# A two-layer mixture of experts on one core: expert 0's rows chosen ahead of the full choice, gate ahead of up for experts 0 and 31, the last down matrix in two halves

## What is computed

```python
g = argmax(h @ w_group + b_group)              # 4 groups of 8 experts
vals, loc = top_k((h @ w_expert + b_expert)[group g], 2)
gates = softmax(groups)[g] * softmax(vals)
for each token's two experts e:
    y += gate * ((silu(x @ w_gate[e]) * (x @ w_up[e])) @ w_down[e])
```

## Time and profile before

| what | value |
| --- | --- |
| median of 3 runs | 1813.89 us (1813.64 to 1815.15) |
| the profiled execution, its own time | 1813.51 us |
| its span in the profile | 1811.8 us |
| TensorE busy | 1522.4 us (84%) |
| VectorE busy | 931.3 us (51%) |
| ScalarE, GpSimd busy | 166.1 us (9%), 111.8 us (6%) |
| read from memory | 531.89 MB, 297 GB/s over the span |
| TensorE's granted clock, mean of the span | 0.918 |

### The profile page before, as it was taken

One profiled execution on the slowest core, in us unless ns is written; L12 is line 12 of the kernel. 1 busy time (PEld: TensorE's weight loads), 2 busy tenths in 40 slices (PEclk: granted clock), 3 DMA queues, 4 the chain that ended last, 5 costly groups with the idle time before them and its releaser, 6 DMA issues. The chain is left out here.

```text
span 1811.8 us, 32599 instructions
## 1 busy us (share of the span) xinstructions
PE 1522.4 (84%) x14545; PEld 1022.8 (56%) x14545; DVE 931.3 (51%) x1882; ACT 166.1 (9%) x388; POOL 111.8 (6%) x121
## 2 busy tenths in 40 slices
PE   8998858788877799876666666689999999999998
PEld 6655534454444795543333333379699445779843
DVE  5844334543234684433322212388877553886756
...
DMA  9377999999999858899999999926544434435420
GB/s 331 140 311 331 414 384 426 426 427 427 427 427 411 327 192 338 351 426 427 426 426 427 426 428 428 415 102 233 186 165 162 168 107 166 140 117 195 154 92 24
DMA packets 80186, 540.33 MB, mean 298 GB/s; under 512 B 7374, under 2 KB 9486, under 8 KB 54188
## 3 DMA queue, kind: packets, MB, share of 16 engines
...
HBM read 531.89 MB, written 6.29 MB: 297 GB/s over the span
## 5 line engine op out<-in xcount | busy, mean ns | idle before, releaser
L930 PE MATMUL ps<-ring,work 128*32 128x256 f32 x3968 | 323.0, 497 | 233.6 <-DMA ring<-in_moe_w_up 231.0
L930 PEld LDWEIGHTS ps<-ring,work 128*32 128x32 f32 x3968 | 177.5, 142 | 373.6 <-issue 338.9
L2372 DVE TENSOR_TENSOR rowb<-rowb,ps 128x128 f32<-128x128 f32 x64 | 18.4, 287 | 381.8 <-ACT rowb L1740 381.8
L906 PE MATMUL ps<-ring,work 128*128 128x512 f32 x312 | 139.5, 592 | 0.0
L942 PE MATMUL ps<-ring,multi 128*32 128x256 f32 x1920 | 114.7, 379 | 0.1
L906 PEld LDWEIGHTS ps<-ring,work 128*128 128x128 f32 x312 | 59.0, 190 | 72.7 <-issue 72.7
L1440 PE MATMUL ps<-hT,ring 128*128 128x128 f32 x768 | 95.4, 275 | 1.5 <-ACT hT L1655 1.5
L906 PE MATMUL ps<-work 128*128 128x512 f32 x212 | 96.0, 592 | 0.0
L1440 PEld LDWEIGHTS ps<-hT,ring 128*128 128x128 f32 x768 | 90.4, 192 | 2.0 <-ACT hT L1655 2.0
L1740 ACT ACTIVATE rowb<-ps 128x128 f32<-128x128 f32 x64 | 17.7, 277 | 753.4 <-PE ps L930 753.4
L963 PE MATMUL ps<-hres,rowb 128*32 128x256 f32 (+1 forms) x1280 | 86.5, 385 | 0.0
...
## 6 DMA issues: line engine op xcount, KB each, us to landing
...
```

Source lines behind the costliest of these rows:

```text
L906: mm = pe.matmul(ps[:, product_bank[n][i], :], left[:, k, :], right[:, k, :], start=(j == 0 and k == 0), stop=(j == pieces - 1 and k == 1))
L930: mm = pe.matmul(ps[32 * q:32 * q + 32, bank, 0:256].rearrange("p (u n) -> p u n", u=2), x[:, k, :], gu[:, k, :, P * q:P * q + P], start=( ...
L2372: link(V.tensor_tensor(hid[b], silu[b], ps[:, 4 + b, P:2 * P], ALU.mult))
```

## The change

1. **Expert 0 ahead of the choice.** Which rows go to expert 0 is found from the logits alone: group 0 is the largest, and expert 0's logit is at least the second largest of its group. VectorE gets this by `max` (the eight largest of a row), three comparisons and products (signal `choice`, first count). TensorE ranks that one column (`running_ranks`, 3, 2 and 1 columns), VectorE makes expert 0's 0/1 matrix, and only then goes on to the full choice, which is rewritten with `max` and fewer passes. The full ranks and totals (`all_ranks`) stand after expert 0's products on TensorE, and the later ranking on VectorE after expert 0's silu product. Expert 1's rows are now picked after expert 0's down product, and their transpose is the last thing in `route`.
2. **Gate ahead of up.** For experts 0 and 31 `gate_or_up` does the gate product and then the up product, 32 matmuls of 128 columns each instead of 32 of 256 in all. Expert 0's gate slot is released after the gate product (`gate_up` counts one more from there on). Expert 31's gate product no longer waits for the up matrix.
3. **The last down matrix in two halves.** Expert 31's down matrix is loaded by two transfers of 1 MB, and the first half of its product waits for the first alone.
4. `keep_busy` goes from 8 (layer 1: 7) to 1 after the logits, from 4 to none behind the ranks, and from 5 to 3 ahead of expert 31 of layer 0.

```diff
-                    holder[s] = (("down" if kind == "down" else "gate_up") + str(l), e + 1)
+                    holder[s] = (f"down{l}", e + 1) if kind == "down" else (f"gate_up{l}", 1 if (e, kind) == (0, "gate") else e + 2)
...
+                    if (e, kind) == (NE - 1, "down"):
+                        sp.dma_start(dst[:, 0:SLOT // 2], src[:, 0:SLOT // 2]).then_inc(S("early_down"), 16)
+                        dst, src = dst[:, SLOT // 2:], src[:, SLOT // 2:]
                     sp.dma_start(dst, src).then_inc(done, 16)
...
+            def gate_or_up(x, bank, gu, u, chunks=range(DC)):
+
+                for k in chunks:
+                    for q in range(4):
+                        mm = pe.matmul(ps[32 * q:32 * q + 32, bank, P * u:P * u + P], x[:, k, :], gu[:, k, u, P * q:P * q + P],
+                                       start=(k == 0), stop=(k == DC - 1))
+                return mm
...
-                keep_busy(8 if l == 0 else 7)
+                def running_ranks(out_, o, w):
+
+                    for d_ in range(nb):
+                        mm = pe.matmul(out_[:, w * d_:w * nb], (before if d_ == 0 else ones)[:, :], o[:, 0:w * (nb - d_)],
+                                       start=(d_ == 0), stop=(d_ == nb - 1), skip_group_check=True)
+                    mm.then_inc(S(f"ranks{l}"), 1)
+
+                keep_busy(1)
                 pe.wait_ge(*nth(f"choice{l}", 1))
-                o = rowb[:, 800:800 + 32 * nb]
-                for d_ in range(nb):
-                    mm = pe.matmul(ps[:, 6, 32 * d_:32 * nb], (before if d_ == 0 else ones)[:, :], o[:, 0:32 * (nb - d_)],
-                                   start=(d_ == 0), stop=(d_ == nb - 1), skip_group_check=True)
-                mm.then_inc(S(f"ranks{l}"), 1)
-                for j in range(nb):
-                    mm = pe.matmul(ps[:, 7, P:P + 32], ones[:, :], o[:, 32 * j:32 * j + 32], start=(j == 0), stop=(j == nb - 1),
-                                   skip_group_check=True)
-                mm.then_inc(S(f"totals{l}"), 1)
-
-                keep_busy(4)
+                running_ranks(ps[:, 4, 384:384 + nb], tmp_a[:, 64:64 + nb], 1)
                 pe.wait_ge(*nth(f"one_hots{l}", 1))
                 pick_rows(l, blocks, 0)
+
+                def all_ranks():
+
+                    pe.wait_ge(*nth(f"choice{l}", 2))
+                    o = tmp_a[:, 640:640 + 32 * nb]
+                    running_ranks(ps[:, 6, 0:32 * nb], o, 32)
+                    for j in range(nb):
+                        mm = pe.matmul(ps[:, 7, P:P + 32], ones[:, :], o[:, 32 * j:32 * j + 32], start=(j == 0), stop=(j == nb - 1),
+                                       skip_group_check=True)
+                    mm.then_inc(S(f"totals{l}"), 1)
+
...
-                        keep_busy(5)
+                        keep_busy(3)
...
-                        for kind in ("gate", "up"):
+                        for kind in ("gate",) if e == NE - 1 else ("gate", "up"):
                             pe.wait_ge(loaded[expert_slots[l, e, kind]], (expert_turn[l, e, kind] + 1) * 16)
...
                     if e == 0:
-                        gate_up(xT[0], 4, gu, range(0, DC // 2))
+                        gate_or_up(xT[0], 4, gu, 0, range(0, DC // 2))
                         pe.wait_ge(*nth(f"xT_ready{l}", 2))
-                        gate_up(xT[0], 4, gu, range(DC // 2, DC)).then_inc(S(f"gate_up{l}"), 1)
-                        pe.wait_ge(*nth(f"one_hots{l}", 2))
-                        pick_rows(l, blocks, 1)
-                        turn_choices()
+                        gate_or_up(xT[0], 4, gu, 0, range(DC // 2, DC)).then_inc(S(f"gate_up{l}"), 1)
+                        gate_or_up(xT[0], 4, gu, 1).then_inc(S(f"gate_up{l}"), 1)
+                        all_ranks()
+                    elif e == NE - 1:
+                        gate_or_up(xT[b], 4 + b, gu, 0)
+                        pe.wait_ge(loaded[expert_slots[l, e, "up"]], (expert_turn[l, e, "up"] + 1) * 16)
+                        gate_or_up(xT[b], 4 + b, gu, 1).then_inc(S(f"gate_up{l}"), 1)
...
                     else:
+                        last = halves_of(ring[:, down_, :])
+                        if e == NE - 1:
+                            pe.wait_ge(*nth("early_down", 48 * (l + 1)))
+                            down(hidT[b], 4 + b, last, range(0, 2))
                         pe.wait_ge(loaded[down_], (expert_turn[l, e, "down"] + 1) * 16)
-                        last = halves_of(ring[:, down_, :])
-                    down(hidT[b], 4 + b, last).then_inc(S(f"down{l}"), 1)
+                    down(hidT[b], 4 + b, last, range(2, 4) if e == NE - 1 else range(4)).then_inc(S(f"down{l}"), 1)
+                    if e == 0:
+                        pe.wait_ge(*nth(f"one_hots{l}", 2))
+                        pick_rows(l, blocks, 1)
+                        turn_choices()
                     if e == 1:
...
                     b = e % 2
-                    act.wait_ge(*nth(f"gate_up{l}", e + 1))
...
+            def inner_rows(l, e):
+
+                b = e % 2
+                dve.wait_ge(*nth(f"silu{l}", e + 1))
+                link(V.tensor_tensor(hid[b], silu[b], ps[:, 4 + b, P:2 * P], ALU.mult))
+                V.transpose(hidT[b].rearrange("p (r s) -> p r s", r=4), by_row(hid[b])).then_inc(S(f"hidT_ready{l}"), 1)
+
+            def turn_rows(l, e):
+
+                dve.wait_ge(*nth(f"rows_picked{l}", e + 1))
+                V.transpose(xT[e % 2], picked_by_row(0, DC)).then_inc(S(f"xT_ready{l}"), 1)
+
...
                 dve.wait_ge(*nth(f"logits{l}", 1))
+                for j in range(nb):
+                    V.max(out=largest[:, j], in_=lo[:, j, NG:NG + EPG])
                 link(V.tensor_reduce(gm, lo[:, :, 0:NG], AX.X, ALU.max))
+                V.tensor_tensor(leads, lo[:, :, 0], gm, ALU.is_ge)
+                link(V.tensor_tensor(first, lo[:, :, NG], largest[:, :, 1], ALU.is_ge))
+                if nb == 3:
+                    V.scalar_tensor_tensor(out=first[:, 0:1], in0=leads[:, 0:1], scalar=first_rows[:, 0:1], in1=first[:, 0:1],
+                                           op0=ALU.mult, op1=ALU.mult)
+                rest = slice(nb - 2, nb)
+                V.tensor_tensor(first[:, rest], first[:, rest], leads[:, rest], ALU.mult).then_inc(S(f"choice{l}"), 1)
+                dve.wait_ge(*nth(f"choice{l}", 1))
+                link(V.tensor_scalar(far, first, -float(P), float(P), ALU.mult, ALU.add))
...
+                dve.wait_ge(*nth(f"ranks{l}", 1))
+                for i in range(nb):
+                    ins = V.scalar_tensor_tensor(out=one_hot[:, i, 0:CAP], in0=ps[:, 4, 384 + i:385 + i].to_broadcast([P, CAP]),
+                                                 scalar=far[:, i:i + 1], in1=iota_e[:, 0:CAP], op0=ALU.add, op1=ALU.is_equal)
+                ins.then_inc(S(f"one_hots{l}"), 1)
...
+                x1, x2 = ix[:, 0:nb], ix[:, nb:2 * nb]
+                for j in range(nb):
+                    ins = V.max(out=largest[:, j], in_=em[:, j])
+                link(ins)
+                for k in range(2):
+                    for j in range(nb):
+                        ins = V.scalar_tensor_tensor(out=at_least[:, k, j], in0=em[:, j], scalar=largest[:, j, k:k + 1],
+                                                     in1=from_end, op0=ALU.is_ge, op1=ALU.mult)
+                link(ins)
+                dve.wait_ge(*nth(f"rows_picked{l}", 1))
+                for c in (0, DC // 2):
+                    V.transpose(xT[0][:, c:c + DC // 2, :], picked_by_row(c, DC // 2)).then_inc(S(f"xT_ready{l}"), 1)
+                link(V.tensor_reduce(x1, at_least[:, 0], AX.X, ALU.max))
+                for j in range(nb):
...
+                link(V.tensor_reduce(x2, at_least[:, 1], AX.X, ALU.max))
+                link(V.tensor_tensor(o12[:, 1], own, wide(x2, NE), ALU.is_equal))
                 V.tensor_tensor(both, o12[:, 0], o12[:, 1], ALU.add).then_inc(S(f"choice{l}"), 1)
...
-                dve.wait_ge(*nth(f"ranks{l}", 1))
...
+                inner_rows(l, 0)
+
+                dve.wait_ge(*nth(f"ranks{l}", 2))
...
-                V.tensor_tensor(one_hot[:, 0:nb, 0:CAP], picked[:, 0], picked[:, 1], ALU.add).then_inc(S(f"one_hots{l}"), 1)
                 one_hots(l, slice(CAP, P))
 
...
-                V.tensor_tensor(choices[:, 0:nb, 3], p1, vexp, ALU.mult).then_inc(S(f"choices_ready{l}"), 1)
+                V.tensor_copy(choices[:, 0:nb, 0:2], slots_left[:, 0:nb, :]).then_inc(S(f"choices_ready{l}"), 1)
...
+                turn_rows(l, 1)
```

84 lines of the change are left out of this document (38 added, 46 removed).

## The result

| kernel | runs | median us | lowest to highest |
| --- | --- | --- | --- |
| before | 8 | 1815.30 | 1813.17 to 1818.44 |
| changed | 8 | 1804.65 | 1801.07 to 1811.18 |

The ratio is 0.9945, with an interval from 0.9933 to 0.9957: 7.8 to 12.2 us faster. The forecast was 1805.6 us, 8.3 us faster. The profiled execution of the changed kernel happened to be its slowest, 1811.18 us, only 2.3 us under that of before. So the two profiles can't be compared by their spans; the stages have to be taken apart first.

A forecast was written before the change was run, and what follows sets the result against it. The prediction took the arrival of the experts' weights as the bound, with gains only before and after that stream. Fronts 1.45 + 2.85 and tails 1.2 + 2.8 make 8.3 us: 1813.9 − 8.3 = 1805.6 us, range 1802 to 1809.

The forecast's parts named there:

- The bound: Both mixtures of experts: each lasts as long as its weights take to arrive, DMA share 1.01 at 421 GB/s.
- Expert 0's chain in layer 0: From VectorE seeing the logits to expert 0's products: they start at 136.7 us instead of 141.28.
- the rival in which the clock never falls: TensorE after the logits keeps full clock: sum 14.6 us, 1799.3 us; chance 0.13.
- A half product: Expert 0's gate or up product alone: 2.15 us at full clock, 3.9 us assumed for gate at 1.2 GHz.
- the rival at 3.66 us: Gate and up products: a half costs as much as the whole; sum 2.9 us, 1811.0 us; chance 0.20.
- the slower rival: Expert 1's products end too late for expert 3's load: sum −5.8 us, 1819.7 us; chance 0.07.
- T1: End of expert 1's products, when expert 3's gate load is issued: 153.35 us in layer 0, 741.15 in layer 1.
- the fronts: Gains ahead of each layer's weight stream from an earlier expert 0: 1.45 us in layer 0, 2.85 in layer 1.
- The rule: Front gain per layer: old issue of expert 2's gate plus 9.8 us, less T1 (154.8 − T1, 744.0 − T1).
- The second hole: New stop in the DMA stream, between expert 2's early loaded gate and up and expert 3's gate.
- The first hole: DMA stream nearly idle while the router works, until expert 2's gate load: 8.6 us in layer 0, 6.5 in layer 1.
- The tails: Expert 31's products after the weight stream end sooner: 1.2 us in layer 0, 2.8 in layer 1.

The follow-up runs named there:

- the front alone: The change with expert 31 as in the kernel before and five fillers; run twice: ratio 0.9941 (1804.86 us), then 0.9964 (1805.55 us).
- the delay: Four fillers added ahead of expert 1's gate_up, in the kernel before (1815.56 us, ratio 1.0002) and in the changed kernel (1808.19 us, ratio 0.9954).
- the second profile: The changed kernel itself, nothing edited, run and profiled once more: 1802.54 us, ratio 0.9936.

## Why the prediction was right

**The bound** held: the stream is as full as before (421 GB/s from 158 to 575 us), and what was won lies in front of it and behind it.

**Expert 0's chain in layer 0**, each step counted from where VectorE sees the logits: ranks start at 1.04 us (1.04 predicted), the round trip took 1.55 (1.5), from the pick to the transposes 3.09 (3.0, with 1.2 for the low clock), the products start at 6.67 (6.5). A `max` of 8 elements took 0.11 us (0.1 taken). The assumption on which this rests, 1.2 GHz until the gate product, is what the rows show (0.50 granted to 142 us). So the rival in which the clock never falls did not come.

**A half product** took 1.95 us at full clock (2.15 taken) and 3.6 at half (3.9). So a half costs half, and the rival at 3.66 us falls. The row of 64x64 tiles was the right neighbour. One reading of the prediction was off: it took 6.08 us for the whole product at half the clock, but two halves at 3.6 make 7.2, and the granted clock from 1159.4 to 1165.5 us was 0.59, not 0.50. Only the slower rival's price and layer 1's tail hung on it.

The Trainium skill's page "TensorE: Matmul & The Clock Gate", section "Back-to-back issue gap", puts a matmul of 128 columns at about 81 ns in a stream of weight loads and matmuls. The prediction's 5.2 us is an estimate from it that counts each of the 64 records as a matmul; with 32 matmuls of two records it would be 2.6 us. The rows show 64 records in 1.95 us, 30 ns a record or 61 ns a matmul, so here the measurement decides against either.

**T1** was the step that was mis-sized. Predicted 23.1 and 20.0 us after the logits, measured 22.1 and 18.7. In layer 0 the products started 0.2 us later than forecast and took 5.33 us instead of 6.05, and T1 followed their end after 10.07 us instead of 10.6, with a little less at each step. In layer 1 they started 0.3 us later and took 4.91 us instead of 6.05, and T1 followed after 8.9 us instead of 9.4:

```profile
723.19 4.91 PE L941 MATMUL ps<-ring,work 128*32 128x128 f32 x128 [0.51 <-DVE work L2175]
```

So the fronts, at 1.45 and 2.85 us, were put too low: alone they measure 2.8 and 3.5.

**The rule** "old issue plus 9.8 less T1" gives, with the measured T1 of the front alone, 24.6 − 22.1 = 2.5 and 22.85 − 19.35 = 3.5 us; measured 2.8 and 3.5. The second hole that it needs is in the windows, and the delay showed the slack ahead of it. The first hole shrank by 4.5 us in layer 0 (issue at 10.3 instead of 14.8 us after the logits), and not that but 2.8 was gained. The rule is not exact: it takes a load as free as long as it comes before the engines run dry, and the windows show up to 1 us lost there. So T1 is not the only thing that counts; with the same T1, the early release moved layer 0's mixture by 1.1 to 1.6 us. And in layer 1 of the change the rule failed by about 2 us: T1 there came 0.6 us sooner than in the front alone and won nothing with it.

**The tails** were put at 1.2 and 2.8 us; alone they measure 1.2 and 1.4, 3.4 and 2.6. In sum 8.3 us were predicted, 9.7 and 10.2 measured in the mixtures and 10.65 in the medians. By layer the forecast was 2.65 and 5.65 us, the measured gain 4.8 and 5.4 (4.7 and 4.9 in the second profile). That layer 1 came out so near is in part luck: T1 came 1.3 us sooner than forecast, and the rule gave about 2 us more for it than was gained.

**Expert 1 too late**, the rival on the slower side, did not come: both halves together took 5.3 and 4.9 us, against its limits of 7.5 and 8.9, and T1 stayed ahead of the old issue plus 9.8 us.
